# Placement of the feed-forward operands, and order and placement of the compression matmuls, in a four-layer hybrid block on one core

## The reference

```python
def compress(t, pos, w):
    blocks = t[:, :, tok] + pos          # 15 blocks of 32 tokens, 64 features, 2 groups
    return blocks.reshape(B, G, n_cmp, CMP_LEN * dh) @ w   # 2048 -> 64

kc = compress(kvh(k_c), cmp_pos[0], cmp_w[0])
vc = compress(kvh(v_c), cmp_pos[1], cmp_w[1])
...
D_FF = 4 * D_MODEL      # hidden = relu(rmsnorm(x) @ w1) ** 2, then hidden @ w2
```

## Time and profile before

| | |
|---|---|
| median of 3 runs | 932.37 us (931.89 to 933.35) |
| the profiled execution | 932.37 us |
| its span, first to last instruction | 930.6 us |
| outside the span | 1.8 us |
| instructions | 13,989 |
| mean granted TensorE clock | 0.998 of full |
| PE matmul busy | 904.6 us |
| DVE busy | 625.5 us |
| ACT busy | 488.0 us |
| DMA | 154.58 MB, 166 GB/s in the mean |

### The profile page before, as it was taken

How to read it: one execution, slowest core, us unless ns; L and a number is a source line. 1 busy time by engine, 2 the same in 40 slices (tenths; PEclk the granted TensorE clock), 3 DMA queues, 4 the chain that set the end, 5 groups by cost and what they waited for, 6 DMA issues and landing times.

```text
span 930.6 us, 13989 instructions
## 1 busy us (share of the span) xinstructions
PE 904.6 (97%) x5688; PEld 773.1 (83%) x5688; DVE 625.5 (67%) x1079; ACT 488.0 (52%) x732; POOL 38.3 (4%) x66
## 2 busy tenths in 40 slices
PE   9999999999999999988999999999998999999998
PEld 7987788887788887866999988878776799998886
DVE  5469978778888897775766654456677586665441
ACT  6545746646655855463655543346576365554330
POOL 2400010000000001000000000000000000000000
PEclk9999999999999999999999999999999999999999
DMA  8842363642245559550555565556463256655540
GB/s 298 301 145 91 99 202 115 225 135 91 92 148 169 180 200 271 153 146 15 167 183 182 194 207 187 184 179 207 155 204 113 91 181 188 192 196 195 183 157 23
DMA packets 79199, 154.58 MB, mean 166 GB/s; under 512 B 5543, under 2 KB 7879, under 8 KB 79136
## 3 DMA queue, kind: packets, MB, share of 16 engines
q1 hardware_dynamic: 75120, 142.81, 46.6%
q0 software_dynamic: 3872, 10.81, 4.7%
q10 hardware_dynamic: 144, 0.07, 0.0%
HBM read 152.57 MB, written 1.11 MB: 165 GB/s over the span
## 4 chain that ended last, share of the span: by engine, by line
PE 74%; DVE 14%; ACT 8%; issue 3%; DMA 0%; SPq 0%; DVEq 0%; ACTq 0%
PE ps L723 15%; PE ps L725 15%; PE ps L724 15%; PE ps L754 7%; PE ps L755 7%; PE ps L756 7%; DVE w_lo L1826 5%; ACT w_hi L1346 3%; PE ps L1028 1%; DVE area L2172 1%; DVE area L2308 1%; DVE area L2096 1%; ACT y_tok L1477 1%; PE ps_mid L1203 1%; ACT area L1564 1%
## 5 line engine op out<-in xcount | busy, mean ns | idle before, releaser
L1826 DVE TENSOR_TENSOR w_lo<-w_raw,w_hi 128x2048 fp32r<-128x2048 f32 (+1 forms) x134 | 302.3, 2261 | 187.1 <-ACT w_hi L1346 187.0
L1346 ACT ACTIVATE w_hi<-w_raw 128x2048 fp32r<-128x2048 f32 (+1 forms) x134 | 252.9, 1890 | 201.1 <-PE ps L725 147.2
L723 PE MATMUL ps<-w_hi,act_hi 128*128 128x512 f32 (+1 forms) x456 | 182.1, 399 | 2.2 <-ACT area L1364 1.0
L725 PE MATMUL ps<-w_hi,act_lo 128*128 128x512 f32 (+1 forms) x456 | 175.0, 384 | 0.0
L724 PE MATMUL ps<-w_lo,act_hi 128*128 128x512 f32 (+1 forms) x456 | 174.7, 383 | 0.0
L723 PE MATMUL ps<-w_hi,hid 128*128 128x512 f32 x296 | 116.1, 392 | 1.0 <-ACT area L1364 0.5
L725 PE MATMUL ps<-w_hi,hid 128*128 128x512 f32 x296 | 115.3, 389 | 0.0
L724 PE MATMUL ps<-w_lo,hid 128*128 128x512 f32 x296 | 115.2, 389 | 0.0
L754 PE MATMUL ps<-act_hi,w_hi 128*128 128x256 f32 x384 | 110.6, 288 | 0.4 <-DVE act_lo L2018 0.4
L755 PE MATMUL ps<-act_lo,w_hi 128*128 128x256 f32 x384 | 107.5, 280 | 0.0
L756 PE MATMUL ps<-act_hi,w_lo 128*128 128x256 f32 x384 | 107.5, 280 | 0.0
(11 more groups left out here) (356 smaller groups left out, 1231.5 us busy)
## 6 DMA issues: line engine op xcount, KB each, us to landing
w_raw<-in_ffn_w SPq DMA_DIRECT2D x64, 1024.0 KB, 5.3
w_raw<-in_w_in SPq DMA_DIRECT2D x22, 1024.0 KB, 5.5
w_raw<-in_a_w_qkv SPq DMA_DIRECT2D x18, 1024.0 KB, 5.0
w_raw<-in_b_w_qkv SPq DMA_DIRECT2D x12, 1024.0 KB, 5.1
w_raw<-in_w_out SPq DMA_DIRECT2D x8, 1024.0 KB, 5.0
w_raw<-in_b_w_o SPq DMA_DIRECT2D x4, 1024.0 KB, 5.0
w_raw<-in_w_in SPq DMA_DIRECT2D x8, 256.0 KB, 6.2
w_raw<-in_w_in SPq DMA_DIRECT2D x4, 512.0 KB, 3.5
```

The source lines that it names most:

```text
L723: pe.matmul(o, ah, wh, start=first, stop=False)
L725: mm = pe.matmul(o, al, wh, start=False, stop=last)
L1346: act.activation(w_hi[:, c % RING, :, 0:n], w_raw[:, c % RAW, :, 0:n], ACT.Copy).then_inc(w_hi_done, 1)
L1826: dve.tensor_tensor(lo, w_raw[:, c % RAW, :, 0:n], hi.bitcast(F), ALU.subtract).then_inc(w_lo_done, 1)
```

## The change

It has two parts.

1. The moving operands of `up0` and `up1` are moved by 8 elements. `early_acts` becomes a tensor of its own without the 8 elements ahead, and tiles 4 to 7 are read and written as `act_hi[:, k, :]` and `act_lo[:, k, :]`. In the allocated program all these tiles then start at a multiple of 512 bytes. ACT and DVE write the tiles at their new place. No instruction and no semaphore is added or taken away.
2. The compression writes both results to partitions 0 to 31 of `ps7`, keys in columns 0 to 63 and values in columns 64 to 127, and it takes the 16 matmuls of the keys first and then the 16 of the values. DVE's second copy reads partitions 0 to 31 instead of 32 to 63.

```diff
-        early_room = sb("early_acts", [128, 2056], FR)
-        sb("area_rest", [128, AREA - 16384 - 2056])
+        early_acts = sb("early_acts", [128, 2, 4, S], FR)
+        sb("area_rest", [128, AREA - 16384 - 2048])
...
-        up_hi, up_lo = [v.rearrange("p k n -> p (k n)")[:, 3 * S + 8:7 * S + 8].rearrange("p (k n) -> p k n", n=S) for v in (act_hi, act_lo)]
-        early_acts = early_room[:, 8:2056].rearrange("p (a k n) -> p a k n", a=2, n=S)
...
             if i < 2 and a in (FFN0_U, FFN1_U):
                 return early_acts[:, 0, 2 * i:2 * i + 2, :], early_acts[:, 1, 2 * i:2 * i + 2, :]
-            if a in (FFN0_U, FFN1_U):
-                return up_hi[:, 2 * i - 4:2 * i - 2, :], up_lo[:, 2 * i - 4:2 * i - 2, :]
             return act_hi[:, 2 * i:2 * i + 2, :], act_lo[:, 2 * i:2 * i + 2, :]
...
-                        ah, al = act_hi[:, k, :], act_lo[:, k, :]
-                        if d["use"] == "relu2":
-                            ah = early_acts[:, 0, k, :] if k < 4 else up_hi[:, k - 4, :]
-                            al = early_acts[:, 1, k, :] if k < 4 else up_lo[:, k - 4, :]
+                        early = k < 4 and d["use"] == "relu2"
+                        ah = early_acts[:, 0, k, :] if early else act_hi[:, k, :]
+                        al = early_acts[:, 1, k, :] if early else act_lo[:, k, :]
...
-                for m in range(16):
-                    for v in range(2):
-                        mm = pe.matmul(ps7[32 * v:32 * v + 32, 64 * v:64 * v + 64], blk[:, v, m, :], cw[:, v, m, :], start=m == 0, stop=m == 15)
+                for v in range(2):
+                    for m in range(16):
+                        mm = pe.matmul(ps7[0:32, 64 * v:64 * v + 64], blk[:, v, m, :], cw[:, v, m, :], start=m == 0, stop=m == 15)
...
-                dve.tensor_copy(v_c[0:32], ps7[32:64, 64:128]).then_inc(cmp_tok, 1)
+                dve.tensor_copy(v_c[0:32], ps7[0:32, 64:128]).then_inc(cmp_tok, 1)
```

## The result

| | before | after |
|---|---|---|
| median | 932.44 us (931.89 to 933.35, 4 runs) | 938.06 us (936.58 to 938.55, 4 runs) |
| ratio | | 1.0065, 95% interval 1.0049 to 1.0081 |
| the profiled execution | 932.37 us, span 930.6 | 939.41 us, span 937.6 |

The forecast was 938.7 us, in a range of 935.9 to 941.5. The profiled execution of after is 1.35 us above its median; the last two sections say what such spread is made of. One thing in the description of the change has to be put right: the tiles 0 to 3 of `up0` and `up1` moved by 8 elements, but tiles 4 to 7 moved from `3 * S + 8` to `4 * S`, by 248 elements. What both have in common is that they stood 32 bytes behind a multiple of 512 and now stand at one.

The account below looks back on a forecast made before the run. The prediction took the length of PE's stream as the bound. Span 930.6 us plus 5.1 for the addresses and 1.2 for the compression made 936.9, with 1.8 outside the span 938.7 us; range 935.9 to 941.5.

Parts of the forecast that it names:

- The stage bound: In up0 and up1 PE is busy throughout the windows at full clock, so matmul start distance sets the time.
- PE never waits there: In up0 and up1 there is no wait to hide in, so all +5.1 us is on the path.
- Part 1: In up0 and up1, tiles at multiples of 512 bytes raise the distance from 116.7 to 120.0 ns: +5.1 us.
- The first rival: In up0 and up1 the address does nothing: 933.6 us, or 935.9 if none of the compression is hidden; 13%.
- Part 2: Compression passes run alone, 55 ns each: +1.76 us a layer, partly hidden, making +1.2 us in all.
- The two rows that priced it: Compression: one pass's float32 stream needs 54 ns, two weight loads 52 ns; loads as the limit would mean +0.
- to be hidden: PE's wait at L1221 absorbs 1.05 us in layer 0 and 1.25 in layer 1, leaving growth of 0.71 and 0.51.
- the distance from the last group ahead to the reader: Ahead of L1221, the last group is through issuing some 0.22 us after its start.
- DVE's L2072: Behind the compression, it waits for L925's scores and goes from 64.05 to about 65, still ahead of later ACT work.
- The sum: Whole kernel: span 930.6 + 5.1 + 1.2 = 936.9, plus 1.8 us outside it, gives 938.7 us (+0.7%).

Follow-up runs that it names:

- both moved: Kernel before with w_hi and w_lo 32 bytes behind a multiple of 512, up tiles left 32 bytes behind one, old compression: 946.45 us against 932.05, ratio 1.0154.
- the weights moved: Kernel before with up tiles at multiples of 512 bytes and w_hi, w_lo 32 bytes behind one, old compression: 944.21 us against 932.05, ratio 1.0134.
- part 2 alone: Kernel before with only the compression's new loop order, result place and copy; up tiles not moved: 933.63 us against 932.05, ratio 1.0021.
- part 1 alone: Kernel before with only the up tiles moved to multiples of 512 bytes; compression as before: 936.78 us against 932.05, ratio 1.0048.
- 256 bytes: Kernel before with the up tiles 256 bytes behind a multiple of 512 in place of 32; one execution, 937.24 us against 932.29.
- 64 bytes: Kernel before with the up tiles 64 bytes behind a multiple of 512 in place of 32; one execution, 932.35 us against 934.24.

## Why the prediction was right

**The stage bound.** That PE's stream is the bound in the `up` stages held: in both stages PE stayed busy for the whole window, and the added time appeared nearly in full, 2.52 and 2.37 us where 768 x 3.3 ns are 2.53. "PE never waits there" was a little too strong: `up1` has one wait inside it, next paragraph.

**Part 1.** Forecast +5.1 us, 3.3 ns for each of 1,536 matmuls. Measured 4.9 us between the stages' ends in the two profiles, and 4.7 us (3.4 to 5.6, by the ratio's interval) in the kernel with this part alone. The step that carried it was to compare the same instruction at two addresses inside one trace, 120.0 ns in the `lru` stretch against 116.7 in `up0`, and to believe that the address was the difference. It was the right reading, but the reason behind it was too simple, and that it gave the right size is in part luck. I spoke of the tile's own address at a multiple of 512 bytes. The runs show that it is the offset against the weights; the `lru` tiles and the new `up` tiles happen to stand alike against them, which I had not asked. With the weights 32 bytes on, the same edit of the `up` tiles is the step from the kernel with both moved to the one with the weights moved, 946.45 to 944.21 us: there it makes the kernel faster. In `up1` 0.15 us less came than in `up0` for the same count; PE's wait at the second half of the tiles, on DVE, was 0.42 us before (at 755.99) and is 0.32 after (at 760.71), which is 0.10 of it.

**The first rival.** "SBUF — State Buffer", section "SBUF: two separate sides", of the Trainium skill says that PE never waits on anyone at its ports. I had made its outcome, 933.6 us, a rival with 13%. The kernel with new addresses and nothing else is 4.7 us slower, so the measurement decides against that outcome: a start address does change the distance. Whether the sentence itself is wrong is not shown. It speaks of the engines against each other, and the likely partner here is PE's own reading of weights, to which the section's table gives an independent port; if that is the partner, the table is what the runs contradict, for fp32r operands.

**Part 2.** Forecast +1.76 us of stream a layer, measured 1.78. The two rows that priced it, 54 ns for 64 columns of float32 against 52 ns for two loads, lay near each other in number and far apart in outcome; the argument that the stream's 54 ns is needed in any case chose rightly. Of it I took 1.05 and 1.25 us to be hidden, and the growth at the reader to be 0.71 and 0.51; measured 0.82 and 0.63. The mis-sized term is the distance from the last group ahead to the reader: I took 0.22 us and it is 65.02 - 64.70 = 0.32. DVE's L2072 was expected at about 65 and came at 65.14, and nothing grew behind it: from the first reader to layer 1's compression it is 135.45 us before and after (64.07 to 199.52, 65.02 to 200.47). The kernel with this part alone is 1.6 us slower, forecast 1.2.

**The sum.** 938.06 us against 938.7. Between marks close to the edits the profiles give 4.9 and 1.45 us: the first term was 0.2 too high and the second 0.25 too low, so the sum is nearer than its terms. They make 6.3 us, and the medians of four executions each rose by 5.6; the last section has a comparison that comes nearer to 6.3. The profiled execution has 0.6 us more between layer 1's compression and `up0` than the two parts explain, at the same mean clock of 0.998. Half is PE's wait for ACT in front of the first `L719` behind the layer's loads, 1.08 us where before has 0.77; this wait has 0.21 and 1.04 us in the kernels with one part alone. The other 0.3 us lie behind it, where after has a wait of 0.32 us (at 432.93) that before has not. No run ties either to the change. The kernel with part 2 alone has 1.8 us less there than before, which the last section explains.

## What to carry to other kernels

Where PE never waits, divide a long window by its count for each kind of matmul and compare kinds that have the same shape: a difference of a few nanoseconds is a term that no list of instructions shows, and here operand addresses alone set it. The offset that is best has to be measured for each form: moving 256 columns against 128 stationary wanted 32 bytes, moving 512 wanted none. The small matmuls on separate partitions ran two at a time only where they stood next to each other in the stream, and the step that nearly doubled cost only what exceeded the wait that its first reader had anyway.

## What the hardware showed that I had not expected

**Equal addresses help one form and hurt the other.** 120.0 against 116.7 ns for the feature form, 227.0 against 233.2 for the token form, at the same two offsets of 0 and 32 bytes. For the token form 32 bytes to either side are alike, for the feature form they are not (116.7 and 118.3). Why the sense turns is open.

**A stretch at half clock, in some executions.** Windows of 430 to 440 us, in the attention before `dswo`, in the profile of before and in that of the kernel with part 2 alone:

```profile
430.00:440.00 10.00, 9.99 (x57) 0.84 0.01 2
```
```profile
430.00:440.00 10.00, 8.97 (x58) 1.00 0.01 2
```

The first fell from 2.4 to 1.2 GHz for a part of the window, with 0.50 in each microsecond from 430 to 433, the second did not, though both had the same 1.26 us wait of PE, which ended at 429.82 and at 430.71. In before the clock fell in this wait (1.00 from 429.00 to 429.40, 0.50 from 429.80 on); in after, where the wait ended at 431.73, it fell later, with 0.50 from 434 to 436. The starts of the first `L723` after the layer's loads and of `up0`, first of before, then of part 2 alone:

```profile
371.39 0.50 PE L723 MATMUL ps<-w_hi,act_hi 128*128 128x512 f32 x1 [0.77 <-ACT area L1364]
...
448.31 0.36 PE L754 MATMUL ps<-early_acts,w_hi 128*128 128x256 f32 x1 [0.32 <-issue]
```
```profile
372.26 0.50 PE L723 MATMUL ps<-w_hi,act_hi 128*128 128x512 f32 x1 [0.21 <-ACT area L1364]
...
447.99 0.36 PE L754 MATMUL ps<-early_acts,w_hi 128*128 128x256 f32 x1 [0.32 <-issue]
```

Between the two, before takes 76.92 us and the other 75.73: the half clock costs 1.2 us, and the wait in front of the first varies by another 0.56. Other profiles agree: with the half clock there the distance is 77.01 (part 1 alone), 76.91 (256 bytes) and 77.25 us (after), without it 75.76 (64 bytes, 370.95 to 446.71). Together clock and wait are as large as part 2.

The times of whole executions fall into groups by the mean granted clock. Of the 17 executions of before beside the first experiments, five with 1.000 take 930.9 us in the mean, nine with 0.998 take 932.1 and three with 0.996 take 934.0. The 27 executions of after on record with these three clocks take 937.3, 938.3 and 940.1 us. At equal clock the change costs 6.1 to 6.4 us, near the 6.3 of the marks, though the two sets were not taken together. That 0.996 is a second such stretch is likely but not shown, as no profile here has that clock.

A single profile of this kernel can't tell an effect under 2 us by its end; it can by the distance between two marks close to the edit.
